# Layer norms with a float32r shift, and small moves in the issue order of two attention mixers

## The reference, cut to what matters

```
for i in range(DEPTH):                                   # DEPTH = 2
    x = LN(alpha*x + 0.5*swiglu(x, ffn1...))
    y = swa_mixer(x, ...) if i == 0 else nsa_mixer(x, ...)
    x = LN(alpha*x + y)
    x = LN(alpha*x + mem_cross_attention(x, mem, ...))
    x = LN(alpha*x + 0.5*swiglu(x, ffn2...))

def layer_norm(x, g, b):
    mu = jnp.mean(x, -1, keepdims=True)
    var = jnp.mean(jnp.square(x - mu), -1, keepdims=True)
    return (x - mu) * lax.rsqrt(var + LN_EPS) * g + b
```

## Time and profile before

| | |
|---|---|
| median of three runs | 2191.91 us |
| the profiled run | 2191.08 us |
| its span | 2189.3 us |
| TensorE busy | 2167.1 us (99%) |
| VectorE / ScalarE / GpSimd busy | 61% / 49% / 36% |
| DMA | 207.5 MB, 95 GB/s |
| mean granted TensorE clock | 0.996 |
| TensorE in the chain that ended last | 93% of the span |

### The profile page before, as it was taken

How to read it: one execution, slowest core, us unless ns; L and a number is a source line. 1 busy time by engine, 2 the same in 40 slices (tenths; PEclk the granted TensorE clock), 3 DMA queues, 4 the chain that set the end, 5 groups by cost and what they waited for, 6 DMA issues and landing times.

```text
span 2189.3 us, 35422 instructions
## 1 busy us (share of the span) xinstructions
PE 2167.1 (99%) x13654; PEld 1921.7 (88%) x13654; DVE 1334.9 (61%) x2315; ACT 1063.5 (49%) x1919; POOL 780.2 (36%) x573
## 2 busy tenths in 40 slices
PE   9999999999999999999999999999999999999998
PEld 8999998878888989898899999887778888989896
DVE  7666666464346938385756666657655346747475
ACT  5435345563445525254643444466654445535353
POOL 3201117557647030305420201555548555120203
PEclk9999999999999999999999999999999999999999
DMA  4333334213313323233232333320004312333332
GB/s 157 116 96 98 106 117 132 78 42 116 117 37 106 108 95 114 90 114 120 85 121 91 101 103 117 115 87 21 21 10 135 106 51 75 116 97 100 103 102 73
DMA packets 58199, 207.50 MB, mean 95 GB/s; under 512 B 6960, under 2 KB 7088, under 8 KB 57264
## 3 DMA queue, kind: packets, MB, share of 16 engines
q1 hardware_dynamic: 56016, 197.68, 29.0%
q10 hardware_dynamic: 2016, 7.55, 0.9%
HBM read 203.10 MB, written 2.10 MB: 94 GB/s over the span
## 4 chain that ended last, share of the span: by engine, by line
PE 93%; DVE 3%; ACT 1%; POOL 1%; issue 1%; DMA 0%; DVEq 0%; ACTq 0%
PE bank L1748 15%; PE bank L1749 14%; PE bank L1750 14%; PE bank L1959 11%; PE bank L1961 11%; PE bank L1960 11%; PE bank L2157 2%; PE bank L2118 2%; PE bank L2090 1%; PE bank L2091 1%; PE bank L1848 1%; PE bank L1849 1%; PE bank L1850 1%; PE bank L1767 1%; PE bank L1778 1%
## 5 line engine op out<-in xcount | busy, mean ns | idle before, releaser
L612 POOL TENSOR_TENSOR w_lo<-w_raw,w_hi 128x1024 fp32r<-128x1024 f32 (+1 forms) x226 | 530.4, 2355 | 1179.2 <-ACT w_hi L789 1179.1
L1748 PE MATMUL bank<-h_hi,w_hi 128*128 128x512 f32 x960 | 381.0, 397 | 2.5 <-DVE h_lo L1552 1.1
L1749 PE MATMUL bank<-h_lo,w_hi 128*128 128x512 f32 x960 | 374.4, 390 | 0.0
L1750 PE MATMUL bank<-h_hi,w_lo 128*128 128x512 f32 x960 | 374.0, 390 | 0.0
L789 ACT ACTIVATE w_hi<-w_raw 128x1024 fp32r<-128x1024 f32 (+1 forms) x227 | 230.5, 1021 | 128.3 <-PE bank L1750 92.4
L1959 PE MATMUL bank<-x_hi,w_hi 128*128 128x256 f32 x864 | 245.2, 284 | 0.3
L1960 PE MATMUL bank<-x_lo,w_hi 128*128 128x256 f32 x864 | 244.5, 283 | 0.0
L1961 PE MATMUL bank<-x_hi,w_lo 128*128 128x256 f32 x864 | 244.5, 283 | 0.0
L1748 PEld LDWEIGHTS bank<-h_hi,w_hi 128*128 128x128 f32 x960 | 180.4, 188 | 47.6 <-issue 4.7
L1750 PEld LDWEIGHTS bank<-h_hi,w_lo 128*128 128x128 f32 x960 | 180.2, 188 | 38.5
L1749 PEld LDWEIGHTS bank<-h_lo,w_hi 128*128 128x128 f32 x960 | 180.5, 188 | 36.1 <-issue 1.9
(11 more groups left out here) (306 smaller groups left out, 5708.1 us busy)
## 6 DMA issues: line engine op xcount, KB each, us to landing
w_raw<-w_dram SPq DMA_DIRECT2D x315, 512.0 KB, 3.5
w_raw<-w_dram SPq DMA_DIRECT2D x64, 448.0 KB, 3.3
f<-mem_dram ACTq DMA_DIRECT2D x5, 1024.0 KB, 6.5
out_dram<-t SPq DMA_DIRECT2D x8, 256.0 KB, 2.2
t<-x_dram SPq DMA_DIRECT2D x2, 512.0 KB, 6.7
f<-cmp_w_dram ACTq DMA_DIRECT2D x1, 1024.0 KB, 5.0
t<-x_dram ACTq DMA_DIRECT2D x2, 256.0 KB, 5.4
t<-x_dram ACTq DMA_DIRECT2D x1, 512.0 KB, 8.0
```

The lines of the kernel that those rows point to most:

```text
L612: pool.tensor_tensor(w_lo[:, slot(s), 0:n * P], w_raw[:, s % RAW, 0:n * P], w_hi[:, slot(s), 0:n * P].bitcast(F32), ALU.subtract).then_inc ...
L1748: pe.matmul(dst, w_hi[:, slot(s), w], m_hi[:, k, :], start=k == 0, stop=False)
L1749: pe.matmul(dst, w_hi[:, slot(s), w], m_lo[:, k, :], start=False, stop=False)
L1750: last = pe.matmul(dst, w_lo[:, slot(s), w], m_hi[:, k, :], start=False, stop=k == n - 1)
```

## The change

The first chunk is rounded on ScalarE to a float32r tile `lead` (a part of `pt`) once `out_free` is up (`lead_round`, new), and the shift multiplies it by `ones8` in float32r. In the mixers and cross attentions the shift is issued after slab 2 instead of slab 1. The `warm(8)` after the seventh norm is `warm(5)`. In swa the output chunks move from n = 55, 56, 57, 58, 60, 62 to 56, 57, 58, 59, 60, 62. In nsa the one at n = 129 moves to 128; the first two chunks of the third query product ("q2") move from n = 12 to 13; the first of the last two turns comes one unit earlier. The wait on `add` after the last unit leaves out the last unit.

```
-WITHIN = {"swa": (-1, 0, 1, 2, 4, 6), "nsa": (-10, -7, -6, -3, 7, 10, 13)}
+WITHIN = {"swa": (0, 1, 2, 3, 4, 6), "nsa": (-10, -7, -6, -3, 7, 9, 13)}
...
-                        self.turn(p, br, g, parts, need + lag + late, need)
+                        soon = p == 7 and br == "win" and j == 0
+                        self.turn(p, br, g, parts, need + lag + late - soon, need)
...
-                    at = (2, 2, 4, 4, 5, 5, 6, 7)[k] if p == 0 else max(b + NSA_Q[k], 12 + k // 2)
+                    at = (2, 2, 4, 4, 5, 5, 6, 7)[k] if p == 0 else max(b + NSA_Q[k], 13)
...
+        lead = pt[:, 0, :]
...
-        ones8 = sb("ones8", [P, P])
+        ones8 = sb("ones8", [P, P], F32R)
...
                         feed(st.out[part][j] + 3)
+                        if not after and j == 0:
+                            lead_round(st)
...
+            def lead_round(st):
+
+                act.wait_ge(out_free, out_reads(st, len(st.out) - 1, 0))
+                act.activation(lead, t[:, 0, :], ACT.Copy).then_inc(lead_ready, 1)
...
             def out_squares(st, load=None):
                 for j in range(KC):
+                    if j == 0:
+                        lead_round(st)
                     feed(st.out[0][j] + 3)
                     square_chunk(st, j)
...
-                    warm(8)
+                    warm(5)
...
-                pe.wait_ge(out_free, out_reads(st, len(st.out) - 1, 0))
-                pe.matmul(bank[B_SHIFT][:], ones8[:], t[:, 0, :], start=True, stop=True).then_inc(shift_ready, 1)
+                pe.wait_ge(lead_ready, st.ln + 1)
+                pe.matmul(bank[B_SHIFT][:], ones8[:], lead, start=True, stop=True).then_inc(shift_ready, 1)
...
-                    if j == 1 and part == len(st.out) - 1:
+                    if j == (1 if st.kind == "ffn" else 2) and part == len(st.out) - 1:
                         shift(st)
...
-                        pe.wait_ge(z["add"], M.n)
+                        pe.wait_ge(z["add"], M.n - 1)
```

More of the change, by code:

```diff
@@ L419, in build @@
         out_free = sem("out_free")
+        lead_ready = sem("lead_ready")
         shift_ready = sem("shift_ready")
@@ L616, in _ @@
             pool.memset(ones[:], 1.0 / D).then_inc(pool_set, 1)
-            pool.memset(ones8[:], 8.0 / D).then_inc(pool_set, 1)
+            pool.memset(ones8[:].bitcast(F32), 8.0 / D).then_inc(pool_set, 1)
             pool.memset(one, 1.0).then_inc(pool_set, 1)
```

## The result

The changed kernel takes 2199.22 us, the median of 6 runs (2197.17 to 2200.34), beside 2191.93 for the kernel before (6 runs, 2190.52 to 2194.28). The ratio is 1.0031, with an interval of 1.0021 to 1.0041: 7.3 us slower. The prediction said 2194.3 and a range to 2197.2. The result lies above the range. The profiled run took 2199.31 us, with a span of 2197.5, 8.2 more than before.

A forecast was written before the change was run, and what follows sets the result against it. TensorE, busy 99% of the span, was taken as the bound. The terms -3.8 + 4.9 - 0.3 + 0.7 + 1.0 + 0.7 - 0.8 gave +2.4 us, 2194.3 on the median; range 2187.6 to 2197.2.

The forecast's parts named there:

- Slab 3 behind the waiting copy: Ends of both mixers: slab 3's rounding and remainder come late behind the shift's copy on ScalarE; +2.4 each, +4.9 together.
- the values behind VectorE's copies at unit 55: swa, output chunks one unit later: values still wait for VectorE's copy of a turn, three products remain to do; +0.7.
- at unit 12: nsa, third query product later: values wait for VectorE's copy of a turn, six products remain to do; +1.0.
- the chunk at 128: nsa, chunk moved from unit 129: delays unit 129's scores and what TensorE waits for after them; +0.7.
- the wait without the last unit: nsa, after the last unit: TensorE's wait of 0.57 us goes; -0.8.
- the six shifts: Feed-forwards and cross attentions: float32r shift and next product take 0.46 instead of 1.09 us, copy hidden; -3.8 together.
- the last two turns: First turn moved earlier: the second ends where it did, so the values' wait stays; 0, at best -1.0.
- A: Rival: slab 3 is not late in the mixers, which then give -0.8 each; 2187.8, chance 0.10.
- B: Rival: the moved chunks pay, as the values after them are not held by VectorE; 2188.3, chance 0.12.
- the cross attentions' slab 4: Cross attentions: rounding of slab 4 comes later but just in time; no stall, 0, up to +0.3 each.
- rival D: After the seventh norm: with fewer ones the granted clock falls once more, +1.7; 2196.0, chance 0.05.
- The ones: After the seventh norm: fewer products of ones end 0.75 earlier, but the next products then wait for `x_lo`; -0.3.

The follow-up runs named there:

- experiment 2: Changed kernel with the first chunks of nsa's third query product back at unit 12: 2198.07 us beside 2191.16 for the kernel before.
- experiment 4: Changed kernel with ten fp32 products of ones in the wait ahead of the values at nsa unit 12: 2197.32 us beside 2191.16 for the kernel before.
- experiment 1: Changed kernel with ScalarE's rounding of slab 3 ahead of the copy for the shift in both mixers: 2189.16 us beside 2191.16 for the kernel before.
- experiment 7: Kernel before with only the float32r shift, placed after slab 2 in mixers and cross attentions, slab 3's rounding first: 2186.61 us beside 2191.83.
- experiment 5: Changed kernel with ten products of ones in nsa unit 12's wait and eleven behind the shift in each mixer: 2194.79 us beside 2191.83 for the kernel before.
- experiment 3: Changed kernel with the swa output chunks back at units 55 to 62: 2198.17 us beside 2191.16 for the kernel before.
- experiment 6: Changed kernel with slab 3's rounding first and third query product, swa chunks and nsa chunk moved back: 2185.48 us beside 2191.83, again 2184.90 beside 2191.32.

## Why the prediction was wrong

**The steps on the queues were right.** Slab 3 behind the waiting copy (forecast +2.4 in each mixer, measured 2.5 and, with slab 4, 2.85), the values behind VectorE's copies at unit 55 (+0.7, 0.6 at full clock) and at unit 12 (+1.0, 1.0), the chunk at 128 (+0.7, 0.7), the wait without the last unit (-0.8, -0.8), the six shifts (-3.8, -3.9), and the last two turns (0, 0). With the clock held up, the kernel's span is 2.5 above before; the sum said 2.4, a nearness that is in part luck, as said above. Rivals A and B are excluded by the waits, and the cross attentions' slab 4 had no stall.

**The step that failed is the clock,** rival D. It read: "with fewer ones the granted clock falls once more after the seventh norm", and had 0.05. A fall was looked for only where the rows of before already showed one. There it is absent in the changed kernel's trace, and in experiments 2 and 4 it came and cost nothing against before. The sum's other terms put four stretches into the program in which TensorE waits 1.4 to 2.9 us, two of them where it had waited 1.1 and 1.5 before, and then priced the work behind each at 0.23 us a product: the clock's answer to these waits was put at nothing, without a reason. The trace shows 0.43 behind three of the four, 5.7 us in all. D's price for one fall, 1.7, was about right (1.3, 1.6, and 2.8 for the longer one); its place and number were wrong. Three falls of 1.7 on top of the sum would have given 2199.4, but that is hindsight: no row of before says which waits fall. In the trace of before the clock stays up behind the 1.5 us at unit 12; three later traces of the same wait have a fall there.

**Sizes that were off.** The mixers' term lacked slab 4: +0.37 each, from rebuilds of 1.73 instead of 1.27. The gain of a shift in a mixer without the late slab was taken as 0.8 and is 0.6 (experiments 1 and 7). The ones were to give -0.3, which they do at half clock, and gave 0 at full clock; the 0.80 that the ones no longer fill is the wait for `x_hi`, which in the rows of before was hidden behind ones at half clock.

**What stays open.** That the extra 5.7 us of the changed kernel's trace are half clock is shown by the rows. That the waits bring the falls, and not something else in the changed kernel, rests on the filled waits (0 falls of 6 in the traces; 4.4 us and a mean clock from 0.9942 to 0.9973 in experiment 5) and on experiment 1. Undoing one step alone (2, 3) moved neither the clock nor, clearly beyond its step, the median. Why a fall comes at one wait and not at the same wait of another run is not settled, so a single place's fall can't be predicted.

## What to carry to other kernels

When an engine's queue is in order, put a new instruction that waits behind the ones that don't: one line on ScalarE, ahead instead of behind, was worth 9 us here. On a kernel that TensorE bounds, price a new wait of the size seen here (1.4 to 2.9 us) twice, once for its own time and once for a fall of the clock that may come behind it (1.1 to 2.9 us each here, in most of the traces but not in all), and look at the mean granted clock over several runs before reading anything into one trace. Where a wait couldn't be removed, small products without a reader in it cost nothing here and kept the clock up.

## What the runs showed of the hardware that was not expected

- The granted clock went to the 1.2 GHz level behind waits of 2.75 and 2.92 us, at one place behind a wait of 1.51 us (experiments 6 and 7), and at one behind waits of 1.44 and 0.57 us with two transposes between. It did so in some traces and not in others with the same instructions.
- The same kernel's runs differ in their mean clock (before: 0.995 to 0.998). Its runs at 0.996 and those at 0.997 took 2192.1 us in the mean, those at 0.998 took 2190.1.
- The start differs too: the same products, with the same instructions ahead of them, began between 24.94 and 27.80 us into the span.
- Products of ones in fp32, 128 by 128 by 128, about 0.12 us a row, filled three waits without moving their ends, and with them the mean clock was 0.9973 instead of 0.9942.
- GpSimd's addition of two 128 by 512 tiles took 1.73 us beside additions of VectorE with both inputs in SBUF and 1.27 to 1.30 otherwise. Its 128 by 1024 subtraction took 2.36 to 2.43 beside instructions of VectorE with one input in a bank, and 2.67 to 2.69 for slab 4 in the kernel before and in experiment 1, where two additions with both inputs in SBUF lie beside it.
